# Every second tile of x scaled by GpSimd instead of VectorE while x is loaded and turned

## The reference, cut to what matters

```python
def rms_norm(x, g):
    xf = x.astype(jnp.float32)
    y = xf * lax.rsqrt(jnp.mean(xf * xf, axis=-1, keepdims=True) + EPS)
    return (y * g.astype(jnp.float32)).astype(x.dtype)
...
    h = rms_norm(x, lp['norm1_g']) * (1 + sc1) + sh1
    proj = h @ lp['w_in']
```

## Time and profile before

| what | value |
|---|---|
| time, median of 3 runs (lowest to highest) | 1665.17 us (1663.81 to 1667.37) |
| the profiled execution's own time | 1663.99 us |
| its span, first to last instruction | 1662.2 us |
| TensorE busy | 1549.1 us, 93% |
| VectorE busy | 976.1 us, 59% |
| ScalarE busy | 646.2 us, 39% |
| GpSimd busy | 292.7 us, 18% |

### The profile page before, as it was taken

The page is one execution under the profiler, slowest core; times in us unless marked ns, Lnnn a source line. Parts: engine busy times, 40 slices in busy tenths (PEclk is TensorE's granted clock), DMA queues, the critical chain, the costliest instruction groups (busy, mean ns, idle before and its releaser), DMA issues.

```text
span 1662.2 us, 22284 instructions
## 1 busy us (share of the span) xinstructions
PE 1549.1 (93%) x8277; PEld 1284.3 (77%) x8277; DVE 976.1 (59%) x1456; ACT 646.2 (39%) x874; POOL 292.7 (18%) x214
## 2 busy tenths in 40 slices
PE   4899999999998889999999999999998499999975
PEld 3688888788887667777777888887887488888852
DVE  6498433055534377778777754333455767777627
ACT  5122121221123465556555632111222167676723
POOL 1021111132224100000000000000000135555420
PEclk9999999999998999999999999999999599999997
DMA  9236343310101010003100033327003269999965
GB/s 381 87 113 223 138 176 135 126 67 25 36 19 61 28 46 1 0 0 120 49 0 0 32 128 132 135 73 241 38 39 140 84 212 274 272 270 275 248 144 233
DMA packets 52732, 199.44 MB, mean 120 GB/s; under 512 B 8507, under 2 KB 17579, under 8 KB 41281
## 3 DMA queue, kind: packets, MB, share of 16 engines
q1 hardware_dynamic: 42432, 173.36, 28.9%
q0 software_dynamic: 10240, 25.28, 7.6%
HBM read 157.03 MB, written 44.63 MB: 121 GB/s over the span
## 4 chain that ended last, share of the span: by engine, by line
PE 32%; DVE 12%; ACT 7%; DMA 7%; issue 5%; POOL 1%; SPq 1%; DVEq 0%; POOLq 0%; ACTq 0%
PE psum L1537 7%; PE psum L1667 4%; DMA xg<-h2d,x_row 4%; PE psum L1607 4%; ACT prob L1764 3%; PE psum L1688 3%; PE psum L1671 2%; DVE rmax L1995 2%; PE psum L1616 2%; DVE rmax L1992 2%; PE psum L1493 1%; DVE rmax L1990 1%; ACT pT_hi L1770 1%; PE psum L1577 1%; DVE pT_lo L2002 1%
## 5 line engine op out<-in xcount | busy, mean ns | idle before, releaser
L349 PE MATMUL psum<-h_hi,w_hi 128*128 128x512 f32 (+1 forms) x768 | 199.3, 368 | 9.8 <-DVE h_lo L770 5.5
L349 PE MATMUL psum<-h_lo,w_hi 128*128 128x512 f32 (+1 forms) x768 | 194.2, 362 | 0.0
L349 PE MATMUL psum<-h_hi,w_lo 128*128 128x512 f32 (+1 forms) x768 | 193.0, 360 | 0.0
L2002 DVE TENSOR_TENSOR pT_lo<-psum,pT_hi 128x512 fp32r<-128x512 f32 x192 | 126.2, 686 | 60.1 <-ACT pT_hi L1770 60.1
L349 PEld LDWEIGHTS psum<-h_hi,w_hi 128*128 128x128 f32 x768 | 130.3, 192 | 34.2 <-issue 11.3
L349 PEld LDWEIGHTS psum<-h_lo,w_hi 128*128 128x128 f32 x768 | 129.6, 191 | 23.3
L349 PEld LDWEIGHTS psum<-h_hi,w_lo 128*128 128x128 f32 x768 | 128.9, 190 | 23.1
L667 POOL TENSOR_TENSOR w_lo<-w_raw,w_hi 128x1024 fp32r<-128x1024 f32 x32 | 79.3, 2480 | 358.5 <-ACT w_hi L523 358.5
L1770 ACT CAST pT_hi<-psum 128x512 fp32r<-128x512 f32 x192 | 104.6, 589 | 79.6 <-PE psum L1493 79.3
L808 DVE SCALAR_TENSOR_TENSOR ada_junk<-adaT,cs_rows 128x1024 f32<-128x1024 f32 x64 | 86.4, 1350 | 69.2 <-DMA adaT<-in_w_adaT 66.4
L1764 ACT ACTIVATE prob<-psum,nmax,q_scale 128x1536 f32<-128x1536 f32 x64 | 104.6, 1634 | 47.3 <-DVE nmax L1996 47.3
(11 more groups left out here) (357 smaller groups left out, 2889.0 us busy)
## 6 DMA issues: line engine op xcount, KB each, us to landing
gu_raw<-in_w_gu SPq DMA_DIRECT2D x32, 1024.0 KB, 6.4
w_raw<-in_w_in SPq DMA_DIRECT2D x16, 1024.0 KB, 4.8
adaT<-in_w_adaT SPq DMA_DIRECT2D x16, 1024.0 KB, 6.2
dn_raw<-in_w_dn SPq DMA_DIRECT2D x16, 1024.0 KB, 8.3
gates<-gst SPq DMA_DIRECT2D x14, 640.0 KB, 3.1
y_sum<-stage SPq DMA_DIRECT2D x12, 512.0 KB, 5.0
xt<-in_x SPq DMA_DIRECT2D x10, 512.0 KB, 7.3
merged<-gates SPq DMA_DIRECT2D x8, 640.0 KB, 4.0
```

Of the source, the lines that this page charges most:

```text
L349: mm = pe.matmul(psum[:, par_sets[j] + g:par_sets[j] + g + w], a[j][:, k, :], b[:, k, g:g + w], start=(k == 0 and a is w_hi and b is h_hi) ...
L2002: nc.vector.tensor_tensor(pT_lo[b][g % 2][:], psum[:, TP + 512 * b:TP + 512 * b + 512], pT_hi[b][g % 2][:], ALU.subtract).then_inc(s[f"a_t ...
```

## The change

In every pair VectorE now raises a new semaphore, `x_root`, when the pair's inverse root is there, scales the even tile itself, and copies both turned tiles of the pair before out of PSUM. GpSimd, in a new loop ahead of its first `split`, waits for `x_root` and scales the odd tile in place, raising `x_odd`. TensorE waits for `x_odd` at odd tiles and for `x_scaled` at even ones.

```diff
@@ turn_x (TensorE)
-                    pe.wait_ge(s["x_scaled"], t + 1)
+                    pe.wait_ge(s["x_odd" if t % 2 else "x_scaled"], t // 2 + 1)
@@ GpSimd
             def _(pool):
+                for t in range(1, TILES, 2):
+                    pool.wait_ge(s["x_root"], t // 2 + 1)
+                    nc.gpsimd.tensor_scalar(xt[:, t, :], xt[:, t, :], rstd[:, t:t + 1], None, ALU.mult).then_inc(s["x_odd"], 1)
+
                 def split(n, j):
@@ VectorE
                     inverse(rstd[:, h], nsq[:, h], ntmp[:, h])
-                    for u in (t, t + 1):
-                        nc.vector.tensor_scalar(xt[:, u, :], xt[:, u, :], rstd[:, u:u + 1], None, ALU.mult).then_inc(s["x_scaled"], 1)
-                        if t:
-                            dve_out(u - 2)
+                    dve.sem_inc(s["x_root"], 1)
+                    nc.vector.tensor_scalar(xt[:, t, :], xt[:, t, :], rstd[:, t:t + 1], None, ALU.mult).then_inc(s["x_scaled"], 1)
+                    if t:
+                        dve_out(t - 2)
+                        dve_out(t - 1)
                 dve_out(TILES - 2)
                 dve_out(TILES - 1)
```

More of the change, by code:

```diff
@@ L169, in build @@
         s = {}
-        for n in ("eps_r x_ss csq_r csd_st csd_in rs_used consts rope wpool_in icnt_in x_sq x_scaled xT_ps xT_outa xT_outd c_in c_sig c_silu fa_mm fa_rows fa_turn fa_mods ada_mm0 ada_mm1 ada_in0 ada_in1 "
+        for n in ("eps_r x_ss csq_r csd_st csd_in rs_used consts rope wpool_in icnt_in x_sq x_root x_scaled x_odd xT_ps xT_outa xT_outd c_in c_sig c_silu fa_mm fa_rows fa_turn fa_mods ada_mm0 ada_mm1 ada_in0 ada_in1 "
                   "mods_b h_raw h_hi_r h_lo_r w_in0 w_hi0 w_hi1 w_lo0 w_lo1 mm0 mm1 ps_free0 ps_free1 pad0 xp_in xp_used "
```

## The result

| what | before | changed |
|---|---|---|
| median of 16 runs each | 1665.90 us | 1670.32 us |
| lowest to highest | 1660.76 to 1669.78 | 1666.40 to 1676.81 |
| profiled execution, own time / span | 1663.99 / 1662.2 us | 1669.70 / 1667.9 us |

The ratio is 1.0034, 95% interval 1.0024 to 1.0044: slower by 4.0 to 7.3 us. The forecast was 1664.0 in a range of 1662.3 to 1669.0, so it was wrong. What happened is rival 2, a GpSimd scale longer than I took it.

The account below looks back on a forecast made before the run. VectorE was taken to pace the first stage, ScalarE next. Moving five scales to GpSimd, less the semaphore's cost and waits, turned tile 9 at 26.44 instead of 27.65: 1665.17 - 1.2 = 1664.0 us, range 1662.3 to 1669.0.

Parts of the forecast that it names:

- rival 2: GpSimd's odd-tile scale is longer than taken: slower from 1.38 us on, 5.1 us slower at 2.40 (1670.3); chance 0.14.
- What bounds the stage: First stage: VectorE paces it at 3.71 us a pair, 1.26 us behind ScalarE; about this much can be won.
- ScalarE's limit: Fifth pair: ScalarE's root, ready at 22.04, allows VectorE's inverse root at 23.23 at the earliest; 24.46 before the change.
- the 1.3 us that I named as the most: Stage gain with ScalarE setting the pace, if VectorE and GpSimd did not exclude each other; more would prove the forecast wrong.
- The 0.15 us behind the root: VectorE raising `x_root` ahead of its even scale: a gap of 0.15 instead of 0.04 us, +0.11 us a pair.
- G = 1.06: GpSimd's scale of a 128x1024 odd tile, in us, worked out from a one-input cast; range kept 0.95 to 2.40.
- The two exclude each other: GpSimd's scale and VectorE's scale or small operations run strictly in turn; copies from PSUM pass; next root at R + 3.18.
- Who gets in first: Behind each root both scales start nearly together, 0.14 against 0.15 us: a tie; VectorE first was the forecast, chance 0.43.
- Rival 1: GpSimd gets in first behind each root, so VectorE's even scale waits: 2.5 us slower, 1667.7; chance 0.33.
- The first pair: No copies there, so VectorE's small operations wait for GpSimd's scale: next root 3.07 us after the first.
- The stage's end moves the program's end: From the vector products to the program's end: what the stage's end moves, the total moves, 1 to 1.
- rival 3: A later wait takes back the 1.2 us, or TensorE's clock shifts about a microsecond: stays at 1665.2; chance 0.10.

Follow-up runs that it names:

- the short copy with VectorE first: Changed kernel, GpSimd copying odd tiles onto themselves instead of scaling, semaphore raised behind VectorE's scale: 16.30 us from first root to vector products, 1.6 less than before.

## Why the prediction was wrong, step by step

- **What bounds the stage: right.** VectorE, with ScalarE 1.26 us ahead of it as the next limit. When VectorE was really relieved, by the short copy with VectorE first, the fifth root came 12.53 us after the first, where the prediction had 23.31 - 10.70 = 12.61 and ScalarE's limit 12.53, and the stage was 1.6 us shorter. That is over the 1.3 us that I named as the most: this limit held for the roots and left out the 0.37 us won behind the last one.
- **The 0.15 us behind the root: right.** 22.33 to 22.48.
- **GpSimd's scale: the step that failed.** "So the cast at 1024 would be 1.06 us. I take G = 1.06." The cast was the nearest row in form, one input, and the copy at 1024 columns does take 1.04. But the scale took 2.84 alone and 3.38 with its wait. So the wait for the odd tile, which the prediction had off the path, set the pace of the first and the last pair, and VectorE won nothing in between. I had kept the range of 0.95 to 2.40, and called a product of two tensors its upper end, because it reads more. That bound was false too: at 2.5 ns a column GpSimd's scale is slower than its product. The statement of the Trainium skill that one-input work is "roughly line-rate" on GpSimd (GPSIMD Engine Reference, engine selection) fits the copy (1.04 us, beside 0.75 for VectorE's scale of the same size) and not the scale (2.84 us); the measurement decides.
- **The two exclude each other: right in kind, wrong in extent.** Rival 2's sum let GpSimd keep the small operations out for its whole length; with 2.68 us (3.53 - 0.85, from the root) it has tile 9 turned at 20.73 + 5 x 2.68 = 34.1. Measured was 30.75. GpSimd's scale holds in two parts, and most small operations fall between them, so that a middle pair came to 3.75 us instead of 4.69. Two errors of opposite sign made the loss 3 us and not 6.5. That the median, 1670.32, is the very 1670.3 that rival 2 gave for a scale of 2.40 us is luck: it goes with 5.1 us lost in the stage, where 3.04 were.
- **Who gets in first: a tie, as told, and both sides occurred.** VectorE got in first beside GpSimd's scale, and GpSimd got in first with its copy. Rival 1 was real, for a GpSimd instruction that the change did not use.
- **The first pair.** The prediction let TensorE turn tile 1 as soon as it was there. It had not reckoned that the transposes are slow at TensorE's start, nor that tile 1 then delays the copies: 1.42 of the 3.04 us.
- **The stage's end moves the program's end: right, with 1 to 3 us on top** in the totals. By 460 us it was 0.1 and 1.3 us in the two profiled executions of the changed kernel, which rival 3 had as "about a microsecond" from TensorE's clock. The stage's 3.04 us alone, on 1665.17, would have given 1668.2, inside the range and still 4 us from the forecast.
- **The range** reached to 1669.0 although rival 2 alone was worked out up to 1670.3; with 0.14 for rival 2 I left out its longer half. Even for rival 1 the end was too low: 1667.7 and the 2.2 us that the runs lay above their median make 1669.9.

## What to carry to other kernels

An operation that an engine has not yet done in the profile is not bounded by its neighbours in form: time it alone, once, before its place in a pipeline is worked out. When work is shared between VectorE and GpSimd, count the time in which each holds the other. Where VectorE sets the pace, let it raise the semaphore behind its own instruction and not ahead of it, so that it is sure to be first. A hand-over can win little more than the distance to the next engine (1.26 us here, and 1.6 in the kernel with the short copy), and in the last round, where nothing hides it, the longer instruction shows in the time (1.45 of the 3.04 us here).

## What the runs showed of the hardware

- GpSimd, 128 rows in float32, alone: scale 2.84 us for 1024 columns, 1.56 for 512, 0.92 for 256; by a constant 2.77; copy 1.04; product of a tensor with itself 1.89.
- During a 2.84 us scale on GpSimd, VectorE's small scales were held for its first 1.0 us and its last 0.8 us and ran at 0.17 us between; its products of two SBUF inputs were held in the first part only. During a 1.04 us copy on GpSimd a small scale was held to the copy's end (0.92 us). The Trainium skill (SBUF — State Buffer, who interferes with whom) has whoever comes first hold the pair for the whole instruction; the copy agrees, and for GpSimd's scale the rows show two holds, so there the measurement decides.
- Released by the same VectorE instruction, a GpSimd copy got in ahead of VectorE's scale (1.04 and 1.55 us), and a GpSimd scale got in behind it (3.38 and 0.75 us). With the semaphore raised behind VectorE's scale, the copy got in behind it (1.56 and 0.75 us).
- A semaphore raised by an instruction of its own in VectorE's queue, between the root and the scale, left 0.15 us between them instead of 0.04.
- TensorE's sixteen vector products took 1.07 us at a granted clock of 1.00 and 1.93 us at 0.50, its lower level of 1.2 GHz. The clock had fallen while TensorE idled for 8.05 us. At the start of its work eight transposes took 1.97 us against 1.09 later, with the granted clock at 1.00 both times.
